# VectorE's order of score pieces and low halves in two attention stages

## The reference, cut to what matters

```python
def mla_attention(q, k, v):            # 8 heads, 2048 keys, causal, blocks of 128 queries
    ...
        sc = jnp.einsum('bqhd,bkhd->bhqk', qb, k).astype(jnp.float32) * scale
        sc = jnp.where(causal[None, None], sc, -jnp.inf)
        p = jax.nn.softmax(sc, axis=-1).astype(v.dtype)
        return jnp.einsum('bhqk,bkhd->bqhd', p, v)

def dsa_attention(q, k, v, q_idx, k_idx, w_idx, k_top):
    ...
        _, sel = lax.top_k(score, k_top)   # 256 keys for each query, chosen by an index score
    ...
        p = jax.nn.softmax(sc, axis=-1).astype(v.dtype)
        o = jnp.einsum('bqkgj,bqjkd->bqkgd', p, vg)
```

## Time and profile before

| | us |
|---|---|
| median of 3 runs | 3377.59 |
| lowest, highest | 3375.81, 3380.34 |
| the profiled execution | 3379.56 |
| its span, first to last instruction | 3377.7 |
| PE busy | 3145.0 (93%) |
| DVE busy | 2081.9 (62%) |
| ACT busy | 1822.9 (54%) |

### The profile page before, as it was taken

How to read it: one execution, slowest core, us unless ns; L and a number is a source line. 1 busy time by engine, 2 the same in 40 slices (tenths; PEclk the granted TensorE clock), 3 DMA queues, 4 the chain that set the end, 5 groups by cost and what they waited for, 6 DMA issues and landing times. The chain is left out here.

```text
span 3377.7 us, 51228 instructions
## 1 busy us (share of the span) xinstructions
PE 3145.0 (93%) x17304; PEld 2641.0 (78%) x17304; DVE 2081.9 (62%) x5122; ACT 1822.9 (54%) x3613; POOL 776.7 (23%) x1078
## 2 busy tenths in 40 slices
PE   7999879999979999997899997999989999869998
PEld 5888768888868777776667776999878888769997
DVE  5767668888845666564899886534446666632112
ACT  5565556676756766663777774211246666632121
POOL 6444411011012122232211001101034444311110
PEclk8999989999989999998899998999999999979999
DMA  4666664436152222225511103544432222244332
GB/s 172 201 200 200 201 137 90 95 71 142 57 196 78 75 86 78 82 79 125 138 43 31 31 20 99 175 132 132 167 124 69 74 74 56 62 144 127 124 125 75
DMA packets 307188, 370.46 MB, mean 110 GB/s; under 512 B 24800, under 2 KB 251936, under 8 KB 303088
## 3 DMA queue, kind: packets, MB, share of 16 engines
q1 hardware_dynamic: 293728, 320.77, 32.7%
q0 software_dynamic: 13200, 46.42, 4.3%
HBM read 216.32 MB, written 150.80 MB: 109 GB/s over the span
## 5 line engine op out<-in xcount | busy, mean ns | idle before, releaser
L93 PE MATMUL i_p_g<-i_hT_lo,i_wh 128*128 128x512 f32 x768 | 308.2, 401 | 9.3 <-DVE i_wl L1639 9.3
L95 PE MATMUL i_p_g<-i_hT_hi,i_wh 128*128 128x512 f32 x768 | 306.0, 398 | 0.0
L94 PE MATMUL i_p_g<-i_hT_hi,i_wl 128*128 128x512 f32 x768 | 306.0, 398 | 0.0
L1657 DVE SCALAR_TENSOR_TENSOR i_score<-i_relu,i_w,i_score 128x1024 f32<-128x1024 f32 (+7 forms) x154 | 155.2, 1024 | 166.6 <-ACT i_relu L1542 164.7
L1552 ACT ACTIVATE i_above<-i_score,i_less 128x2048 bf16<-128x2048 f32 (+13 forms) x140 | 183.1, 1308 | 104.5 <-POOL i_less L1609 67.6
L1081 DVE TENSOR_TENSOR mla_tl<-mla_p_t,mla_th 128x512 fp32r<-128x512 f32 (+1 forms) x320 | 186.1, 606 | 45.3 <-ACT mla_th L1124 41.8
L1124 ACT ACTIVATE mla_th<-mla_p_t 128x512 fp32r<-128x512 f32 (+1 forms) x320 | 163.9, 530 | 86.4 <-PE mla_p_t L1021 83.8
L1081 DVE TENSOR_TENSOR dsa_tl<-dsa_p_t,dsa_th 128x512 fp32r<-128x512 f32 x272 | 180.0, 686 | 42.8 <-ACT dsa_th L1124 36.6
L1051 DVE CUSTOM_DVE_ANT_0 dsa_probs<-dsa_p_s,dsa_mask 128x512 f32<-128x512 f32 (+3 forms) x320 | 184.6, 605 | 16.0 <-PE dsa_p_s L1806 14.5
L1124 ACT ACTIVATE dsa_th<-dsa_p_t 128x512 fp32r<-128x512 f32 x272 | 155.4, 593 | 70.4 <-PE dsa_p_t L1021 69.7
L1542 ACT ACTIVATE i_relu<-i_p_s 128x1024 f32<-128x1024 f32 (+7 forms) x176 | 141.6, 813 | 77.8 <-DVE i_score L1654 39.4
(11 more groups left out here) (337 smaller groups left out, 9667.9 us busy)
## 6 DMA issues: line engine op xcount, KB each, us to landing
scratch_gates<-i_ob SPq DMA_DIRECT2D x95, 256.0 KB, 2.4
m_m<-scratch_gates SPq DMA_DIRECT2D x64, 256.0 KB, 4.0
f_hs<-scratch_h2T SPq DMA_DIRECT2D x16, 1024.0 KB, 9.9
scratch_qkT<-b_th SPq DMA_DIRECT2D x64, 192.0 KB, 2.6
scratch_qkT<-b_tl SPq DMA_DIRECT2D x64, 192.0 KB, 2.9
i_ws<-in_w_in SPq DMA_DIRECT2D x24, 512.0 KB, 4.4
b_xt<-in_x SPq DMA_DIRECT2D x16, 512.0 KB, 4.8
scratch_h<-b_xh POOLq DMA_DIRECT2D x16, 512.0 KB, 3.0
```

The costliest lines, as they stand in the source:

```text
L93: pe.matmul(out, l[0], r[1], start=start, stop=False)
L94: pe.matmul(out, l[1], r[0], start=False, stop=False)
L95: return pe.matmul(out, l[0], r[0], start=False, stop=stop)
L1657: nc.vector.scalar_tensor_tensor(out=acc, in0=r, scalar=w[:, t, h:h + 1], in1=acc, op0=ALU.mult, op1=ALU.add).then_inc(summed, 1)
```

## The change

A new function `blocks_ahead` rewrites the list of steps for VectorE alone. Where a piece of scores is directly ahead of a block (with only `E` or `V` steps between, which VectorE has no share in), the block comes first and the piece after it. A piece is held until the next piece, block or output is seen; if that is a block of an earlier unit, the block overtakes it. The exception in the code, a block of the piece's own unit, does not arise, since blocks are always one unit behind. The lists of TensorE, ScalarE, GpSimd and SyncE stay as they are. 123 pieces of 320 in the MLA stage change places with a block, and 120 of 320 in the DSA stage; 51 and 48 of these are the last pieces of their tile, which make the shift.

```diff
--- before.py
+++ after.py
@@ -903,6 +903,23 @@
     return steps + [("O", n) for n, _ in late]
 
 
+def blocks_ahead(steps):
+
+
+    order, held = [], []
+    for step in steps:
+        if step[0] == "S":
+            order += held
+            held = [step]
+        elif step[0] == "B":
+            order += held + [step] if held and held[0][1] == step[1] else [step] + held
+            held = []
+        elif step[0] == "O":
+            order += held + [step]
+            held = []
+    return order + held
+
+
 def stage_attention(nc, sem, tag, ident, layer, space):
 
 
@@ -1040,7 +1057,7 @@
         def _(dve):
             layer.dve_start(dve)
             i = 0
-            for step in steps:
+            for step in blocks_ahead(steps):
                 if step[0] == "S":
                     _, n, s, ch, k0, w, last = step
                     if ch == 0:
```

## The result

The changed kernel takes 3465.05 us (median, 3462.17 to 3466.52), the kernel before 3377.85 on the same chip. The ratio is 1.0252, with a 95% interval from 1.0239 to 1.0264: 87.2 us slower. The forecast was 3448.1, with a range from 3405 to 3485.

The account below looks back on a forecast made before the run. TensorE was taken to end almost everything in MLA, both TensorE and VectorE near their limit in DSA. Pair losses of 32.9 us in MLA and 37.6 in DSA, together 70.5, gave 3450.1 profiled, 3448.1 median; range 3405 to 3485.

Parts of the forecast that it names:

- pair 18: MLA, 16 pieces and 12 blocks: E1 1.6 us late, B7 2.8 late, the pair 3.3 longer, taken as 3.1.
- the bank: MLA pairs with 16 pieces, 12 blocks: 3.1 taken, a little under 3.3, since TensorE may be in front by a bank.
- three pairs with more blocks between: 2.0 each: DSA pairs with 16 pieces and more blocks between the exponentials: 2.0 us slower each.
- DSA pairs with 12 pieces: Eight pairs, 1.2 us slower each, as MLA pair 17: 0.6 + 0.9 - 0.3.
- single exchanges of MLA: 15 MLA pairs with one exchanged piece: last piece and shift now delay B1, 0.7 us each, between 0 and 0.95.
- the pairs with 4 pieces: Seven DSA pairs with four narrow pieces: 0.3 us slower each.
- upper end of the unknown terms: 16-block pairs and single exchanges at their upper bounds: sum 81 us, time 3459.
- DSA pairs with 8 pieces: Eight pairs: S7 and its shift, 0.84, go behind B0, a 0.20 wait takes up part: 0.64 us each.
- Rival 1: Late shifts partly absorbed, only each pair's first chain counts: half the sum, 35 us, 3413; chance 0.22.
- Rival 2: Clock falls too in 16 DSA pairs with mixed steps, 24 us more, 3472; chance 0.15, shared with a larger sum.
- Rival 3: Faster: TensorE's waits for low halves all go, 10 to 35 us return, 3357 at the middle; chance 0.08.
- Rival 4: No change: three score and three transposed banks absorb a one-step shift, within 6 us of 3377.6; chance 0.05.

Follow-up runs that it names:

- experiments with plain and last pieces: Change narrowed to 144 plain pieces (not last of their tile): 3402.07; to 99 last pieces, which make a shift: 3441.26; kernel before 3377.89.
- that with ScalarE's list: On top of the changed kernel, ScalarE's exponentials of the next unit go behind the following block's high half: 3409.30 against 3379.89 before.
- mla_only: Kernel before, with VectorE taking blocks ahead in the MLA stage alone: 3418.89 against 3377.89, ratio 1.0114.
- pieces_ahead: Kernel before, with VectorE taking a piece ahead of the block in front of it, except at a pair's first block: 3383.47 against 3379.89.
- chosen: Kernel before, with B1 ahead of the last piece in front of it in MLA pairs 4, 12, 20, 28 alone: 3377.76 against 3379.89.
- exps_behind: Alone on the kernel before: ScalarE's exponentials go behind the next block's high half, VectorE's list as before: 3387.78 against 3379.89.
- the kernel with the chosen orders: Kernel before, with block, piece and exponential orders moved only in pairs where earlier runs were shorter: 3373.75 against 3380.83, ratio 0.9980.

## Why the prediction came out as it did

**The mechanism was right, step by step.** In pair 18 the prediction had E1 1.6 us late, B1 2.47 behind it, and 3.3 us for the whole pair, of which 3.1 was taken. The changed kernel has B1 2.46 behind E1 (751.67 to 754.13), 2.50 and 1.97 us idle before B1 and B7 (2.5 and 2 forecast), and 3.08 for the pair, from S0 to S0 as the forecast counted it. So 3.1 was right and 3.3 was not: B7 is 2.74 late against the pair's S0 (2.8 forecast), but the piece behind it adds 0.34 and not 0.6. Whether the bank that was given as the reason for taking 0.2 off has to do with it, no run shows; that part is luck. The two experiments with plain and last pieces separate its two parts, the 0.6 of the piece behind the wait and the late shift; that with ScalarE's list shows the link between them.

**Where the other 14 us are.** The sum was too small, 70.5 us where the profiled executions differ by 84.1. From the first RECIPROCAL row of a stage to its last it is 36.9 us more in MLA (32.9 forecast) and 43.4 more in DSA (37.6); 3.7 lie before the first pair, and 0.3 between the stages. By terms of the sum, forecast and then measured from RECIPROCAL to RECIPROCAL (the start of the next pair can lie up to 0.3 differently, as in pair 18):

| pairs | forecast | measured |
|---|---|---|
| MLA 16 pieces, 12 blocks (4) | 12.4 | 12.8 |
| MLA 16, 16 (4) | 6.4 | 7.9 |
| MLA 12, 8 (4) | 4.8 | 4.8 |
| MLA 12, 16 (4) | -1.2 | -1.1 |
| MLA, one exchange (15) | 10.5 | 12.5 |
| DSA 16 pieces, like pair 23 (5) | 14.8 | 15.1 |
| DSA 16 pieces, more blocks (3) | 6.0 | 9.7 |
| DSA 12 pieces (8) | 9.6 | 12.8 |
| DSA 8 pieces (8) | 5.1 | 2.0 |
| DSA 4 pieces (7) | 2.1 | 3.9 |

The step that failed most is "three pairs with more blocks between: 2.0 each". It rested on the idea, taken over from MLA, that more blocks give VectorE waits of its own to give up. One of these three, pair 29 of DSA, from RECIPROCAL to RECIPROCAL, first the kernel before and then the changed one:

```profile
2005.51:2029.56 24.05, 22.88 (x128) 17.21 (x126) 21.16 (x58) 17.17 (x25) 1.88 (x2) 1.00 0.03 6
```

```profile
2083.05:2110.24 27.19, 23.29 (x127) 17.23 (x126) 21.13 (x59) 17.17 (x24) 1.89 (x2) 1.00 0.03 5
```

VectorE is busy 21.16 of 24.05 us before, and 21.13 of 27.19 after. The 2.89 us between 24.05 and 21.16 were the waits at exponentials (1.41 and 0.91 us) and 0.57 in small gaps, so there was next to nothing to give up, and all of the 3.14 us is new idle time, in these rows of the changed kernel:

```profile
2086.95 0.69 DVE L1098 TENSOR_TENSOR dsa_tl<-dsa_p_t,dsa_th 128x512 fp32r<-128x512 f32 x1 [2.72 <-ACT dsa_th L1141]
...
2097.40 0.69 DVE L1098 TENSOR_TENSOR dsa_tl<-dsa_p_t,dsa_th 128x512 fp32r<-128x512 f32 x1 [2.07 <-ACT dsa_th L1141]
...
2109.63 0.69 DVE L1098 TENSOR_TENSOR dsa_tl<-dsa_p_t,dsa_th 128x512 fp32r<-128x512 f32 x1 [0.80 <-ACT dsa_th L1141]
```

The blocks between the exponentials are VectorE's own work; they fill the pair and give no slack. The window over the pair in the trace of before would have told it. In the DSA pairs with 12 pieces (1.6 instead of 1.2) the figure of MLA pair 17 was carried over, and the 0.3 taken off for a wait ahead of the next pair's first piece had no counterpart: the earlier trace rows is MLA's, where this wait did go (S0 at 744.88 has none), and in the trace of before VectorE has no such wait in the DSA pairs 15 to 22. Both misses have one sign and one cause: a reserve was deducted that no row of that kind of pair showed.

The other terms were mis-sized by the width of a piece. The single exchanges of MLA came to 0.83 on average, between 0.65 and 1.10, and not 0.7. The 0.84 from which 0.7 was taken is that of a piece of 256 keys with its shift; in these pairs the exchanged piece has 512. How much of its length TensorE took up at the transposes of B4, no run separates. In DSA the loss goes by the width as well: in pairs 9 to 14 it is about 0.6 at 256 keys, 0.7 at 384 and 0.83 at 512, and in the pairs with 4 pieces, called narrow in the prediction and priced at 0.3, it is 0.44, 0.46 to 0.70 and 0.8. The upper end of the unknown terms, given as 81, is 80.2 when added up, which moves nothing.

What is left is not the change's. In the DSA pairs with 8 pieces the 2.0 is 5.2 from the exchanges (5.1 forecast) less 3.2 from the clock (last section). Of the 3.9 in the pairs with 4 pieces 0.65 is pair 1's, which grew by the same in three kernels whose list there was that of before (`mla_only`, `pieces_ahead`, `chosen`). The 3.7 before the first pair go with the clock too. The first RECIPROCAL row stood between 462.1 and 467.5 us in the kernels of this study, and at 462.1 with the last pieces alone, whose lists are the changed kernel's up to there. At the start of the stage the clock was low, and it rose later in the changed kernel. The same three microseconds, before and then changed:

```profile
459.00:462.00 3.00, 3.00 (x18) 2.49 (x17) 2.84 (x11) 1.91 (x5) 0.00 (x0) 0.96 1.15 249
```

```profile
459.00:462.00 3.00, 3.00 (x11) 2.61 (x10) 1.88 (x8) 1.73 (x3) 0.00 (x0) 0.50 1.07 252
```

Without these three (3.7 and 0.65 too much, 3.2 too little) the change costs some 83 us in this pair of executions, and the sum is 12 short of it.

**The rivals.** Rival 1 (absorbed, 3413) is refuted by the time and by the second chain of pair 18; a form of it is true of the MLA pairs with 16 blocks alone. Rival 2 (the clock falls, 3472) is the nearest in time but wrong: the granted clock was 1.00 from 1800 to 2100 us, with TensorE down to 86.07%. TensorE stood 53 times for low halves in MLA and 38 times in DSA, where it had been 20 and 6, and yet the clock stayed at 1.00 in MLA from 465 us on, and in DSA from 1660 to 2133 us, which is in pair 30. By the rule of the Trainium skill ("TensorE: Matmul & The Clock Gate", section "A second HAM failure mode: psum-queue depth-cycling") such short idle spells between groups of matmuls can make the clock swing; the trace of the changed kernel doesn't bear it out. But the mechanism is not absent. With the last pieces alone exchanged, the clock fell once in a DSA pair with 16 pieces, and that pair grew by some 1.8 us more than its neighbour (last section). Two kernels as alike as these differ in it, so that the changed kernel was spared is in part luck. Rival 3 (faster, 3357) needed TensorE's 9.7 us of waits for low halves to go; they tripled. Its mechanism exists in the four pairs with 12 pieces and 16 blocks: it is worth 0.61 us in each alone, and 0.3 is left with the rest of the change. Rival 4 (no change) is refuted by every pair of the table but these.

**The other signs.** The waits for high halves were to reach "90 or more in each stage": 91.0 and 78.9, so DSA's was less. TensorE's busy share was to fall to about 92%: 92 to 94 in windows of 100 us in MLA, 86 to 90 in those of DSA. The stages grew by 36.9 and 43.4 us, where 33 and 38 were forecast.

**What stays open.** With the last pieces alone exchanged, DSA pairs 29 and 30 grew by 4.09 and 3.87 us, more than with the whole change (3.14 and 3.60). In pair 29 the clock fell (last section), which accounts for the excess. In pair 30 the clock was low for about as long in all three kernels, and no run of this study says why the plain pieces give something back there. Nor is it settled what makes the clock fall in some executions.

## What to carry to other kernels

Before you move a step ahead on an in-order engine, look whether its input is there already: otherwise what stood in front of it was the work that filled its wait, and that work now comes late. Look for what the pushed-back step feeds on a third engine (here the shift, then an exponential, ahead of the high half that the moved step needs next); such a ring costs more than the step itself: in pair 18 the last pieces alone put 1.04 us more idle time before B1, for a low half of 0.6 us that went ahead, and with the plain pieces it was 1.66. Deduct slack only where the window over just that pair shows the engine idle for it.

## What the runs showed of the chip

The granted clock does not follow from the list of instructions alone. In the kernel before it fell at the narrow pieces of the DSA stage, and the pairs 7 and 8 there took 10.25 and 11.92 us. The kernel with the change in MLA alone has the same DSA list; at the same place, 41 us later, its windows are:

```profile
1689.00:1692.00 3.00, 2.07 (x10) 1.22 (x10) 2.75 (x16) 1.81 (x5) 0.93 (x1) 1.00 0.29 61
1692.00:1695.00 3.00, 3.00 (x22) 2.60 (x23) 2.57 (x11) 2.36 (x6) 0.00 (x0) 1.00 0.00 0
```

TensorE was busy 2.07 of 3 us, even less than the 2.26 of the earlier trace rows, and yet the clock stayed at 1.00 in these and the next 3 us, where it had been 0.52. Both pairs were 1.6 us shorter. In the changed kernel and in five others of this study it stayed up in both pairs as well. With the last pieces alone, and with `exps_behind` alone, both pairs were as slow as before; in `chosen`, whose DSA list is again that of before, only pair 8 was. So up to 3.2 us of each comparison of profiled executions hang on something that no row here shows. I count them as scatter of single executions and not as an effect of an order.

The same can happen in a long pair. With the last pieces alone exchanged, these are two windows at the start of DSA pair 29, and TensorE's transposes between them:

```profile
2060.00:2063.00 3.00, 1.06 (x8) 0.63 (x7) 0.97 (x4) 3.00 (x5) 0.00 (x0) 0.99 0.00 0
2063.00:2066.00 3.00, 3.00 (x11) 2.50 (x12) 3.00 (x7) 0.64 (x2) 1.80 (x2) 0.50 0.00 0
```

```profile
2062.91 1.10 PE L1038 MATMUL dsa_p_t<-ident,dsa_probs 128*128 128x128 f32 x4 [1.94 <-DVE dsa_tl L1098]
```

TensorE had stood 1.94 us for a low half, the clock then fell to 0.50, and the four transposes took 1.10 us instead of 0.60. The pair grew by 4.09 us, while its neighbour, pair 28, with the same order, grew by 2.31. In the changed kernel TensorE stands 1.94 us at the same place of this pair, and there the clock stayed at 1.00. So neither the list nor the length of the last wait tells a fall.

The 0.65 us of pair 1 and the 0.46 of pair 30 go with the clock as well. Both stages begin with the clock at 0.50. In the DSA stage of the kernel before it was at 1.00 between, from 1613 to 1616 us, and so for about as long in the kernels whose pair 1 kept its length; in the changed kernel it stayed at 0.50 from 1650 to 1659. And at the end of pair 30, where it is low for 2.6 us before, it was so for 0.9 us in `mla_only`, and not at all in the kernel with the chosen orders, whose pair 30 was 0.46 shorter too.
